# The first products of eight stages from the high parts of x alone, ahead of the fourth transposes, and tile 20's down products together ahead of tile 21's

## The chip, the cores and the metric

The kernel runs on one core of one Trainium2 chip. The metric is the device time of one execution in microseconds, lower is better. TensorE is called PE here, ScalarE ACT, VectorE DVE, GpSimd POOL; SP issues the transfers.

## What is computed

A block of the first kind and two of the second, on one sequence of 256 tokens with 1024 features, in float32:

```
x = x + 0.5 * swiglu(rms_norm(x))            # FFN a        norm 0
x = x + hybrid_mixer(rms_norm(x))            # mixer        norm 1
x = x + 0.5 * swiglu(rms_norm(x))            # FFN b        norm 2
x = rms_norm(x)                              #              norm 3
for i in (0, 1):
    # for i = 1: keys and values of MLA from x first (shared_kv)
    x = layer_norm(ALPHA * x + 0.5 * swiglu(x))          # FFN c, e     norms 4, 8
    x = layer_norm(ALPHA * x + mix(x))                   # FoX / MLA    norms 5, 9
    x = layer_norm(ALPHA * x + 0.5 * swiglu(x))          # FFN d, f     norms 6, 10
    x = layer_norm(ALPHA * x + sigmoid(x @ w_gate + b) * (p[i] @ w_proj))   # norms 7, 11

swiglu(x) = (silu(x @ w_gate_half) * (x @ w_up_half)) @ w_down    # hidden width 2752 or 2816
```

## The kernel before

**Split products.** A float32 product is made of three products of rounded operands: a tensor is split into a high part (`_hi`, an ACT copy) and what is left of it (`_lo`, a DVE subtraction), and hi x hi, hi x lo and lo x hi are added in PSUM. This holds for the weights (`w_hi`, `w_lo`, made from the landed `w_raw` by `split_hi` L308 and `split_lo` L315, in pieces of 1024 columns, in places 512) and for the activations.

**Stages.** Every engine has a program of its own, written out in order; semaphores tie them. Norm n ends in a turn: `x` is normalised in four pieces p = 0 to 3 (block b = p % 2 of 128 tokens, half p // 2 of the features), by `dve_rms_apply` (L537) or `dve_ln_apply` (L545, L548). PE transposes each piece with four transposes (`pe_turn`, L367) into banks 4, 6, 5 and 7; ACT copies each bank to `xT_hi` (`act_turn`, L471), DVE makes `xT_lo` (L557). Eight of the norms are followed by a stage whose first step is changed: FFN a to f, the mixer and FoX. In four of them ACT scales the whole of `x` by ALPHA after the fourth copy (`act_scale`, L476) - FFN c, d, e, f - and so it does in FoX.

**An FFN.** 22 tiles of 128 hidden features. `gate_up(i)` makes 48 products of 256 columns (`feature_major`, L343) over the eight k tiles of features; for tile 0 they come in a front (k 0 to 3) and a back half (k 4 to 7). ACT and DVE make the hidden tile from it (`silu` L487, product L575, high L491, low `hT_lo` L577). `down(i)` adds 12 products of 512 columns (`token_major`, L352) onto four accumulators, `psum[2 * b + half]` for block b and half of the features. `down(i - 1)` stands behind `gate_up(i)`, so that the hidden tile is made meanwhile. Behind the FFN, DVE adds each accumulator to `x` (`dve_add`, L524), ACT squares the halves (L457), and DVE and POOL make the factor of the norm (L512, L514, L601).

**Weights.** The chunk of tile i + 1 is split while tile i is worked on. In ACT's order at a stage's start stand: the four copies, the scaling, the last piece of chunk 0 (the down weights), pieces 0 and 1 of chunk 1, then `silu` of tile 0. The other pieces of chunk 0 are split during the stage before, except in FFN a, where they follow the fourth copy.

Of the kernel before, what the change touches and what calls it, by code (L numbers as in the profile page):

```python
# [16 lines left out]
P = 128  # L17
# [192 lines left out]
def build(nc, t, out):  # L210
    with ExitStack() as ctx:
# [149 lines left out]
        def pe_turn(n, src):  # L361
            for p in range(4):
# [7 lines left out]
        def pe_ffn(f, n):  # L370
# [21 lines left out]
            def down(tiles):  # L392
                for b in range(TB):
                    for half in range(2):
                        for i in tiles:
                            c = at + i
                            wait_split(pe, c, GU, FF_COLS)
                            pe.wait_ge(h_lo_made, FF_TILES * f + i + 1)
                            s = i % 2
                            ins = token_major(psum[2 * b + half][:, :], w_hi[chunks[c].pair], w_lo[chunks[c].pair],  # L400
                                              lambda j: GU + 512 * half, 512, (0,), lambda k: hT_hi[s], lambda k: hT_lo[s],
                                              b, i == 0, i == FF_TILES - 1)
                        if len(tiles) == 2:
                            ins.then_inc(acc_made, 1)
                if len(tiles) == 1:
                    ins.then_inc(down_made, 1)
# [40 lines left out]
        def act_squares(n, src, mean, blocks=range(TB)):  # L447

            for b in blocks:
                if n == 0:  # L450
                    act.wait_ge(x_landed[b], 16)
# [99 lines left out]
        def dve_turn(n, apply, eps):  # L551
# [7 lines left out]
            for p in range(4):  # L559
                b, k0 = p % 2, p // 2 * 4  # L560
                if p < 2:
                    dve_mean(n, b, eps)
# [1593 lines left out]
```

## Time and profile before

| | |
|---|---|
| median of 3 runs | 1975.18 us (1971.28 to 1981.16) |
| the profiled execution | 1975.18 us, its span 1973.9 us |
| PE busy | 1798.7 us, 91% of the span |
| DVE busy | 1088.8 us, 55% |
| ACT busy | 887.7 us, 45% |
| HBM | 298.52 MB read, 152 GB/s over the span |

The span is the stretch from the profile's first to its last instruction; the execution's time has 1.3 us around it. A busy share is an average over all stages: an engine that is at 91% may be the bound in most of them and idle at each border between two.

### The profile page before, as it was taken

The numbers are of one execution on the slowest core, as the hardware profiler recorded it, in microseconds if no ns is written. First come the engines' busy times: TensorE is split into PE (matmuls) and PEld (weight loads), VectorE is DVE, ScalarE is ACT, GpSimd is POOL, SyncE is SP. The second block draws the span as 40 slices with busy tenths as digits, with TensorE's granted clock in tenths as the row PEclk, the third lists the DMA queues.
The fourth block names the chain that finished last, engine by engine and source line by source line (L and its number), as shares of the span: only waits on it lengthen the run. The fifth ranks groups of instructions, "written<-read, shape, count | busy, mean of one in ns | idle before, by whom it ended". The sixth has DMA issues, their size and how long they took to land.

```text
span 1973.9 us, 27882 instructions
## 1 busy us (share of the span) xinstructions
PE 1798.7 (91%) x11764; PEld 1608.9 (82%) x11764; DVE 1088.8 (55%) x1696; ACT 887.7 (45%) x1515; POOL 105.1 (5%) x116
## 2 busy tenths in 40 slices
PE   7999897888999899988989999789997888899985
PEld 6999877666999799978868998579997667699974
DVE  5545555994554554554755555564556455455455
ACT  4444543344444444435645444454444444444443
POOL 0000001231000000001210000100000000100000
PEclk9999997999999999999999999889998999899997
DMA  8555340006555455525335554345543222454531
GB/s 318 182 189 182 107 173 33 1 1 242 188 181 189 150 194 190 192 98 192 131 125 197 192 186 177 117 156 192 192 157 141 77 96 75 167 201 181 192 107 43
DMA packets 31964, 301.38 MB, mean 153 GB/s; under 512 B 3792, under 2 KB 4320, under 8 KB 5984
## 3 DMA queue, kind: packets, MB, share of 16 engines
q1 hardware_dynamic: 31840, 299.60, 41.9%
q8 instruction: 93, 1.52, 0.3%
q14 instruction: 31, 0.25, 0.0%
HBM read 298.52 MB, written 1.06 MB: 152 GB/s over the span
## 4 chain that ended last, share of the span: by engine, by line
PE 78%; DVE 13%; ACT 5%; issue 2%; POOL 1%; DMA 0%; SPq 0%; DVEq 0%; ACTq 0%
PE bank L343 44%; PE bank L352 29%; DVE w_lo L315 2%; ACT w_hi L308 1%; DVE x L548 1%; PE bank L367 1%; POOL rstd L601 1%; DVE w_raw L1071 1%; DVE w_raw L1141 1%; DVE xT_lo L557 1%; DVE w_raw L1090 1%; ACT w_raw L913 1%; DVE w_raw L1076 1%; PE bank L787 1%; DVE mla_nm L1266 1%
## 5 line engine op out<-in xcount | busy, mean ns | idle before, releaser
L315 DVE TENSOR_TENSOR w_lo<-w_raw,w_hi 128x1024 fp32r<-128x1024 f32 (+4 forms) x545 | 608.5, 1170 | 386.2 <-ACT w_hi L308 385.5
L343 PE MATMUL bank<-xT_hi,w_hi 128*128 128x256 f32 x2392 | 685.9, 287 | 10.4 <-DVE w_lo L315 8.4
L343 PE MATMUL bank<-xT_lo,w_hi 128*128 128x256 f32 x2392 | 681.9, 285 | 0.0
L343 PE MATMUL bank<-xT_hi,w_lo 128*128 128x256 f32 x2392 | 681.5, 285 | 0.0
L308 ACT ACTIVATE w_hi<-w_raw 128x1024 fp32r<-128x1024 f32 (+4 forms) x561 | 523.7, 996 | 258.1 <-PE bank L352 258.0
L343 PEld LDWEIGHTS bank<-xT_hi,w_hi 128*128 128x128 f32 x2392 | 464.2, 194 | 22.6 <-DVE w_lo L315 10.1
L343 PEld LDWEIGHTS bank<-xT_lo,w_hi 128*128 128x128 f32 x2392 | 464.1, 194 | 5.7
L343 PEld LDWEIGHTS bank<-xT_hi,w_lo 128*128 128x128 f32 x2392 | 463.9, 194 | 0.0
L352 PE MATMUL bank<-w_hi,hT_hi 128*128 128x512 f32 x528 | 208.9, 396 | 7.4 <-DVE hT_lo L577 7.4
L487 ACT ACTIVATE ff_silu<-bank 128x256 f32<-128x256 f32 x132 | 51.0, 387 | 358.2 <-PE bank L343 358.0
L352 PE MATMUL bank<-w_hi,hT_lo 128*128 128x512 f32 x528 | 208.6, 395 | 0.0
L352 PE MATMUL bank<-w_lo,hT_hi 128*128 128x512 f32 x528 | 208.5, 395 | 0.0
L575 DVE TENSOR_TENSOR ff_silu<-ff_silu,bank 128x256 f32<-128x256 f32 x132 | 55.8, 422 | 204.8 <-ACT ff_silu L487 204.6
L352 PEld LDWEIGHTS bank<-w_hi,hT_hi 128*128 128x128 f32 x528 | 99.6, 189 | 28.0 <-issue 9.9
L352 PEld LDWEIGHTS bank<-w_lo,hT_hi 128*128 128x128 f32 x528 | 99.0, 187 | 23.9
L352 PEld LDWEIGHTS bank<-w_hi,hT_lo 128*128 128x128 f32 x528 | 98.9, 187 | 18.0
L352 PE MATMUL bank<-w_hi,xT_hi 128*128 128x256 f32 (+3 forms) x272 | 92.3, 339 | 9.9 <-DVE xT_lo L557 4.8
L577 DVE TENSOR_TENSOR hT_lo<-ff_silu,hT_hi 128x256 fp32r<-128x256 f32 x132 | 56.1, 425 | 64.0 <-ACT hT_hi L491 64.0
L352 PE MATMUL bank<-w_hi,xT_lo 128*128 128x256 f32 (+3 forms) x272 | 91.1, 335 | 0.0
L352 PE MATMUL bank<-w_lo,xT_hi 128*128 128x256 f32 (+3 forms) x272 | 91.0, 334 | 0.0
L601 POOL TENSOR_TENSOR rstd<-rstd,minus_half 128x1 f32<-128x1 f32 x24 | 21.5, 896 | 1288.0 <-DVE rstd L514 1288.0
L491 ACT ACTIVATE hT_hi<-ff_silu 128x256 fp32r<-128x256 f32 x132 | 55.2, 418 | 64.5 <-DVE ff_silu L575 64.5
(290 smaller groups left out, 1887.1 us busy)
## 6 DMA issues: line engine op xcount, KB each, us to landing
w_raw<-in_ffn_a SPq DMA_DIRECT2D x22, 1536.0 KB, 6.8
w_raw<-in_ffn_b SPq DMA_DIRECT2D x22, 1536.0 KB, 6.7
w_raw<-in_ffn_c SPq DMA_DIRECT2D x22, 1536.0 KB, 6.7
w_raw<-in_ffn_d SPq DMA_DIRECT2D x22, 1536.0 KB, 6.6
w_raw<-in_ffn_e SPq DMA_DIRECT2D x22, 1536.0 KB, 6.6
w_raw<-in_ffn_f SPq DMA_DIRECT2D x22, 1536.0 KB, 6.7
gains<-in_gains SPq DMA_DIRECT2D x11, 1024.0 KB, 5.6
w_raw<-in_mla_up SPq DMA_DIRECT2D x8, 1280.0 KB, 5.4
```

Source lines behind the costliest of these rows:

```text
L308: nc.scalar.activation(w_hi[c.pair][:, a:b], raw[c.slot][:, a:b], ACTF.Copy).then_inc(w_hi_made, 1)
L315: nc.vector.tensor_tensor(w_lo[c.pair][:, a:b], raw[c.slot][:, a:b], w_hi[c.pair][:, a:b].bitcast(F32), ALU.subtract).then_inc(w_lo_made, 1)
L343: ins = nc.tensor.matmul(o, w[:, c], a[:, k, :], start=(n == 0), stop=(n == last))
L352: ins = nc.tensor.matmul(o, a(k)[:, tok_of(b)], w[:, c], start=(first_k and n == 0), stop=(last_k and n == 3 * len(ks) - 1))
L367: ins = nc.tensor.transpose(bank[:, i * P:(i + 1) * P], src[:, b, (k0 + i) * P:(k0 + i + 1) * P], ident)
L487: nc.scalar.activation(sig[s][:, :], psum[4 + i % 4][:, 0:SEQ], ACTF.Silu).then_inc(silu_made, 1)
L491: nc.scalar.activation(hT_hi[s][:, :], sig[s][:, :], ACTF.Copy).then_inc(h_hi_made, 1)
L548: nc.vector.scalar_tensor_tensor(xb, xb, rstd[:, b:b + 1], gains[:, D + c.start:D + c.stop], ALU.mult, ALU.add).then_inc(normed, 1)
L557: nc.vector.tensor_tensor(lo, got, hi.bitcast(F32), ALU.subtract).then_inc(xT_lo_made, 1)
L575: nc.vector.tensor_tensor(sig[s][:, :], sig[s][:, :], up[:, SEQ:2 * SEQ], ALU.mult).then_inc(h_made, 1)
L577: nc.vector.tensor_tensor(hT_lo[s][:, :], sig[s][:, :], hT_hi[s][:, :].bitcast(F32), ALU.subtract).then_inc(h_lo_made, 1)
L601: nc.gpsimd.tensor_tensor(rstd[:, b:b + 1], rstd[:, b:b + 1], expo[:, 0:1], ALU.pow).then_inc(rooted, 1)
```

## The change

**At a stage's start** (`pe_first`, called by `pe_ffn` for tile 0 of each FFN, by `pe_mixer` and by `pe_fox`; `pe_turn` is no longer called ahead of these). PE transposes pieces 0, 1, 2. Then it makes, for the front half of the features, all products with `xT_hi`: w_hi and w_lo. Then it transposes piece 3, and makes the front products with `xT_lo`, the back ones with `xT_hi`, the back ones with `xT_lo`. The weights are waited for up to the half in question. The gate of tile 0 goes to bank 2 instead of bank 4, FoX's first tile to bank 0 instead of 6, as transposed pieces still stand in the banks used before. The number of products stays the same.

**In FFN a**, ACT and DVE split the first two pieces of chunk 0 ahead of the third copy and of the fourth normalised piece.

**At an FFN's end**, all of `down(20)`, block 1 first, stands behind `gate_up(21)`, and `down(21)` behind it. Before, tiles 20 and 21 alternated in each accumulator.

**Squares**: ACT waits for each half of a block by itself in norms 1 to 3.

```diff
-        def pe_turn(n, src):
-            for p in range(4):
+        def pe_turn(n, src, pieces=range(4)):
+            for p in pieces:
...
+        def pe_first(n, src, i, tiles):
+            hi, lo = w_hi[chunks[i].pair], w_lo[chunks[i].pair]
+            front, back = range(KD // 2), range(KD // 2, KD)
+
+            def of_high(ks):
+                wait_split(pe, i, 0, len(tiles) * P * (ks[-1] + 1))
+                for j, o in enumerate(tiles):
+                    for k in ks:
+                        c = slice((len(tiles) * k + j) * P, (len(tiles) * k + j + 1) * P)
+                        nc.tensor.matmul(o, hi[:, c], xT_hi[:, k, :], start=(k == 0), stop=False)
+                        nc.tensor.matmul(o, lo[:, c], xT_hi[:, k, :], start=False, stop=False)
+
+            def of_low(ks, signal=None):
+                for j, o in enumerate(tiles):
+                    for k in ks:
+                        c = slice((len(tiles) * k + j) * P, (len(tiles) * k + j + 1) * P)
+                        ins = nc.tensor.matmul(o, hi[:, c], xT_lo[:, k, :], start=False, stop=(k == KD - 1))
+                    if signal is not None:
+                        ins.then_inc(signal, 1)
+                return ins
+
+            def products(signal=None):
+                pe_turn(n, src, (0, 1, 2))
+                pe.wait_ge(xT_hi_made, 4 * n + 2)
+                of_high(front)
+                pe_turn(n, src, (3,))
+                pe.wait_ge(xT_lo_made, 4 * n + 2)
+                of_low(front)
+                pe.wait_ge(xT_hi_made, 4 * n + 4)
+                of_high(back)
+                pe.wait_ge(xT_lo_made, 4 * n + 4)
+                return of_low(back, signal)
+            return products
...
+                if i == 0:
+                    pe_first(n, src, c, (psum[2][:, 0:SEQ], psum[3][:, SEQ:2 * SEQ]))().then_inc(gate_up_made, 1)
+                    return
                 wait_split(pe, c, 0, GU)
-                if i == 0:
-                    for ks in (range(KD // 2), range(KD // 2, KD)):
-                        wait_xT(n, ks)
-                        feature_major(bank[:, 0:SEQ], hi, lo, lambda k: 2 * P * k, KD, xT_hi, xT_lo, ks)
-                        ins = feature_major(psum[3][:, SEQ:2 * SEQ], hi, lo, lambda k: 2 * P * k + P, KD, xT_hi, xT_lo, ks)
-                    ins.then_inc(gate_up_made, 1)
-                    return
...
             for i in range(FF_TILES):
                 gate_up(i)
                 if 1 <= i < FF_TILES - 1:
-                    down((i - 1,))
-            down((FF_TILES - 2, FF_TILES - 1))
+                    down(i - 1, 0)
+                    down(i - 1, 1)[1].then_inc(down_made, 1)
+
+            down(FF_TILES - 2, 1)
+            down(FF_TILES - 2, 0)
+            for b in range(TB):
+                for ins in down(FF_TILES - 1, b):
+                    ins.then_inc(acc_made, 1)
...
         def act_program():
             act_squares(0, x, False)
-            act_turn(0)
-            act_split(first["ffn_a"], 0, 4)
+            act_turn(0, (0, 1))
+            act_split(first["ffn_a"], 0, 2)
+            act_turn(0, (2, 3))
+            act_split(first["ffn_a"], 2, 4)
...
-            dve_turn(0, to_xn, RMS_EPS)
-            dve_split(first["ffn_a"], 0, 4)
+            dve_turn(0, to_xn, RMS_EPS, lambda: dve_split(first["ffn_a"], 0, 2))
+            dve_split(first["ffn_a"], 2, 4)
```

PE's order at the end of FFN b, behind `gate_up(21)`, before the change (`hT_hi0` is tile 20's hidden tile, `hT_hi1` tile 21's; banks 0 to 3 are the accumulators):

```order
L352 MATMUL bank0<-w_hi1,hT_hi0 128x512 [waits h_lo_made]
L352 MATMUL bank0<-w_hi1,hT_lo0 128x512
L352 MATMUL bank0<-w_lo1,hT_hi0 128x512
L352 MATMUL bank0<-w_hi0,hT_hi1 128x512 [waits h_lo_made,w_lo_made]
L352 MATMUL bank0<-w_hi0,hT_lo1 128x512
L352 MATMUL bank0<-w_lo0,hT_hi1 128x512
L352 MATMUL bank1<-w_hi1,hT_hi0 128x512
```

And with the change:

```order
L352 MATMUL bank2<-w_hi1,hT_hi0 128x512 [waits h_lo_made]
...
L352 MATMUL bank3<-w_hi1,hT_hi0 128x512
...
L352 MATMUL bank0<-w_hi1,hT_hi0 128x512
...
L352 MATMUL bank1<-w_hi1,hT_hi0 128x512
L352 MATMUL bank1<-w_hi1,hT_lo0 128x512
L352 MATMUL bank1<-w_lo1,hT_hi0 128x512
L352 MATMUL bank0<-w_hi0,hT_hi1 128x512 [waits h_lo_made,w_lo_made]
```

All 12 products of tile 20 now stand between `gate_up(21)` and the first that waits for tile 21's hidden tile; there were three.

PE's order at the start of FFN c, before (L367 are the transposes, bank 7 holds the fourth piece, banks 4 and 3 tile 0's gate and up):

```order
L367 MATMUL bank5<-const,x 128x128 [waits normed]
L367 MATMUL bank5<-const,x 128x128 x3
L367 MATMUL bank7<-const,x 128x128 [waits normed]
L367 MATMUL bank7<-const,x 128x128 x3
L343 MATMUL bank4<-xT_hi,w_hi1 128x256 [waits xT_lo_made,w_lo_made]
L343 MATMUL bank4<-xT_lo,w_hi1 128x256
L343 MATMUL bank4<-xT_hi,w_lo1 128x256
```

And with the change, from the third transposes (bank 5) on; L381 and L382 are the products of `xT_hi`, L388 those of `xT_lo`:

```order
L367 MATMUL bank5<-const,x 128x128 [waits normed]
L367 MATMUL bank5<-const,x 128x128 x3
L381 MATMUL bank2<-xT_hi,w_hi1 128x256 [waits w_lo_made,xT_hi_made]
L382 MATMUL bank2<-xT_hi,w_lo1 128x256
...
L381 MATMUL bank3<-xT_hi,w_hi1 128x256
L382 MATMUL bank3<-xT_hi,w_lo1 128x256
L367 MATMUL bank7<-const,x 128x128 [waits normed]
L367 MATMUL bank7<-const,x 128x128 x3
L388 MATMUL bank2<-xT_lo,w_hi1 128x256 [waits xT_lo_made]
L388 MATMUL bank2<-xT_lo,w_hi1 128x256 x3
L388 MATMUL bank3<-xT_lo,w_hi1 128x256 x4
L381 MATMUL bank2<-xT_hi,w_hi1 128x256 [waits w_lo_made,xT_hi_made]
```

The fourth transposes stood right behind the third; 16 products, all with the high part, now stand between them.

## Rows read from the trace of the kernel before

**Rows 1.** The page, part 4: the chain that ended last, by engine.

```profile
PE 78%; DVE 13%; ACT 5%; issue 2%; POOL 1%; DMA 0%; SPq 0%; DVEq 0%; ACTq 0%
```

**Rows 2.** The list of waits: engine, line, releaser; us in all, times, longest.

```profile
PE bank L343 <- DVE w_lo L315: 8.4, 5, 4.0
...
PE bank L352 <- DVE hT_lo L577: 7.4, 6, 1.2
```

**Rows 3.** Timeline of PE, end of FFN a: start us, us, what.

```profile
203.05 0.39 PE L352 MATMUL bank<-w_hi,hT_hi 128*128 128x512 f32 x1
...
203.52 0.39 PE L352 MATMUL bank<-w_lo,hT_hi 128*128 128x512 f32 x1
205.15 0.47 PE L352 MATMUL bank<-w_hi,hT_hi 128*128 128x512 f32 x1 [1.24 <-DVE hT_lo L577]
```

**Rows 4.** Timeline, the same FFN: last add and next stage's transposes.

```profile
210.31 0.69 DVE L524 SCALAR_TENSOR_TENSOR x<-bank,x 128x512 f32<-128x512 f32 x1 [0.70 <-PE bank L352]
...
212.81 0.44 PE L367 MATMUL bank<-const,xn 128*128 128x128 f32 x2 [2.55 <-DVE xn L537]
```

**Rows 5.** Timeline of PE, start of FFN c.

```profile
682.28 2.38 PE L367 MATMUL bank<-const,x 128*128 128x128 f32 x8 [1.01 <-DVE x L537]
685.47 1.11 PE L367 MATMUL bank<-const,x 128*128 128x128 f32 x4 [0.81 <-DVE x L537]
686.24 0.56 PE L343 MATMUL bank<-xT_hi,w_hi 128*128 128x256 f32 x1
686.60 0.41 PE L343 MATMUL bank<-xT_lo,w_hi 128*128 128x256 f32 x1
686.81 0.41 PE L343 MATMUL bank<-xT_hi,w_lo 128*128 128x256 f32 x1
...
692.95 0.28 PE L343 MATMUL bank<-xT_lo,w_hi 128*128 128x256 f32 x1
693.07 0.28 PE L343 MATMUL bank<-xT_hi,w_lo 128*128 128x256 f32 x1
693.64 0.35 PE L343 MATMUL bank<-xT_hi,w_hi 128*128 128x256 f32 x1 [0.29 <-DVE w_lo L315]
```

**Rows 6.** Windows table, FFN c: busy us by engine, granted clock, DMA share, GB/s.

```profile
682.30:688.60 6.30, 5.34 (x23) 4.54 (x24) 3.84 (x6) 3.17 (x4) 0.00 (x0) 0.50 0.28 117
```

**Rows 7.** Timeline of ACT, start of FFN c.

```profile
683.44 0.60 ACT L471 ACTIVATE xT_hi<-bank 128x512 fp32r<-128x512 f32 x1 [1.53 <-PE bank L367]
...
686.62 0.60 ACT L471 ACTIVATE xT_hi<-bank 128x512 fp32r<-128x512 f32 x1 [1.32 <-PE bank L367]
687.12 1.90 ACT L476 ACTIVATE x<-x 128x2048 f32<-128x2048 f32 x1
688.92 2.95 ACT L308 ACTIVATE w_hi<-w_raw 128x1024 fp32r<-128x1024 f32 x3
```

**Rows 8.** Timeline of DVE, end of FFN c, ahead of a layer norm.

```profile
873.45 0.69 DVE L524 SCALAR_TENSOR_TENSOR x<-bank,x 128x512 f32<-128x512 f32 x1 [1.12 <-PE bank L352]
...
875.78 0.16 DVE L531 SCALAR_TENSOR_TENSOR minus_mean<-row_sums,minus_mean 128x1 f32<-128x1 f32 x1
...
877.66 0.69 DVE L524 SCALAR_TENSOR_TENSOR x<-bank,x 128x512 f32<-128x512 f32 x1 [0.70 <-PE bank L352]
```

**Rows 9.** Timeline of PE, kernel's start: tile 0 of FFN a.

```profile
18.45 0.55 PE L343 MATMUL bank<-xT_hi,w_hi 128*128 128x256 f32 x1 [4.02 <-DVE w_lo L315]
```

**Rows 10.** Timeline of PE, start of FFN d: third and fourth transposes.

```profile
1038.71 1.12 PE L367 MATMUL bank<-const,x 128*128 128x128 f32 x4 [0.94 <-DVE x L548]
1040.76 1.11 PE L367 MATMUL bank<-const,x 128*128 128x128 f32 x4 [0.93 <-DVE x L548]
```

**Rows 11.** Timeline of PE, start of FFN e: fourth transposes, tile 1.

```profile
1294.56 1.11 PE L367 MATMUL bank<-const,x 128*128 128x128 f32 x4 [0.93 <-DVE x L548]
...
1303.11 0.28 PE L343 MATMUL bank<-xT_hi,w_hi 128*128 128x256 f32 x1
```

**Rows 12.** Timeline of PE, FoX: its first product.

```profile
889.66 0.58 PE L343 MATMUL bank<-xT_hi,w_hi 128*128 128x256 f32 x1 [1.41 <-DVE xT_lo L557]
```

More of the change, by code:

```diff
@@ L390, in gate_up, with down @@
                               range(KD)).then_inc(gate_up_made, 1)
[L392 to L406, printed above, removed]
+            def down(i, b):
+                c, s = at + i, i % 2
+                wait_split(pe, c, GU, FF_COLS)
+                pe.wait_ge(h_lo_made, FF_TILES * f + i + 1)
+                return [token_major(psum[2 * b + half][:, :], w_hi[chunks[c].pair], w_lo[chunks[c].pair],
+                                    lambda j: GU + 512 * half, 512, (0,), lambda k: hT_hi[s], lambda k: hT_lo[s],
+                                    b, i == 0, i == FF_TILES - 1) for half in range(2)]
             for i in range(FF_TILES):
@@ L449, in act_squares @@
             for b in blocks:
-                if n == 0:
-                    act.wait_ge(x_landed[b], 16)
-                elif mean:
-                    act.wait_ge(mean_made, 2 * (n - 4) + b + 1)
-                else:
-                    act.wait_ge(added, 4 * (n - 1) + 2 * b + 2)
-                for half in range(2):
+                for half in range(2):
+                    if n == 0:
+                        act.wait_ge(x_landed[b], 16)
+                    elif mean:
+                        act.wait_ge(mean_made, 2 * (n - 4) + b + 1)
+                    else:
+                        act.wait_ge(added, 4 * (n - 1) + 2 * b + half + 1)
                     ins = nc.scalar.activation(xn[:, b, half_of(half)], src[:, b, half_of(half)], ACTF.Square,
@@ L465, in turned_views, with act_turn @@
             return [z[:, k0:k0 + 4, tok_of(b)] for z in (xT_hi, xT_lo)] + [bank[:, :].rearrange("p (k t) -> p k t", t=P)]
-        def act_turn(n):
-            for p in range(4):
+        def act_turn(n, pieces=range(4)):
+            for p in pieces:
                 hi, _, got = turned_views(n, p)
@@ L486, in activate @@
                     act.wait_ge(h_lo_made, n0 + i - 1)
-                nc.scalar.activation(sig[s][:, :], psum[4 + i % 4][:, 0:SEQ], ACTF.Silu).then_inc(silu_made, 1)
+                gate = psum[2 if i == 0 else 4 + i % 4]
+                nc.scalar.activation(sig[s][:, :], gate[:, 0:SEQ], ACTF.Silu).then_inc(silu_made, 1)
                 act.wait_ge(h_made, n0 + i + 1)
@@ L562, in dve_turn @@
                     dve_mean(n, b, eps)
+                if p == 3:
+                    before_last()
                 apply(n, b, slice(k0 * P, (k0 + 4) * P))
@@ L690, in pe_mixer @@
         def pe_mixer():
-            i = first["nsa_a"]
-            hi, lo = w_hi[chunks[i].pair], w_lo[chunks[i].pair]
-            for ks in (range(KD // 2), range(KD // 2, KD)):
-                wait_xT(1, ks)
-                wait_split(pe, i, 0, 3 * P * (ks[-1] + 1))
-                for j in range(3):
-                    ins = feature_major(psum[j][:, 0:SEQ], hi, lo, lambda k: (3 * k + j) * P, KD, xT_hi, xT_lo, ks)
-                    if ks[0]:
-                        ins.then_inc(mix_tile, 1)
+            pe_first(1, xn, first["nsa_a"], [psum[j][:, 0:SEQ] for j in range(3)])(mix_tile)
             none = (mix_copied, 0)
@@ L1308, in pe_fox @@
         def pe_fox():
-            wait_xT(4, range(KD))
             none = (fox_tile, 0)
-            pe_features(first["fox_f"], [(psum[6][:, 0:SEQ], none)], fox_tile)
+            pe_first(4, x, first["fox_f"], [psum[0][:, 0:SEQ]])(fox_tile)
             tiles = lambda f0, f1: [(psum[7][:, 0:SEQ], f0), (psum[6][:, 0:SEQ], f1)]
@@ L1365, in act_fox @@
             act.wait_ge(small_landed, 16)
-            nc.scalar.activation(z_f[:, :], psum[6][0:FOX_H, 0:SEQ], ACTF.Identity, bias=small[0:FOX_H, HG + 1:HG + 2]).then_inc(fox_f_made, 1)
+            nc.scalar.activation(z_f[:, :], psum[0][0:FOX_H, 0:SEQ], ACTF.Identity, bias=small[0:FOX_H, HG + 1:HG + 2]).then_inc(fox_f_made, 1)
             act_split(first["fox_v"] + 1)
```

24 lines of the change are left out of this document (8 added, 16 removed).

## Prediction

> **What bounds the kernel now.** I read the page first: the chain that ended last is TensorE for 78% of the span and VectorE for 13% [rows 1]. TensorE (PE) is the bound inside the stages, and time can only be won where it stands idle between them. The list of waits gives the two idle places that the edit touches: six waits of 1.2 us for the last hidden tile, `hT_lo`, one at the end of each FFN, and five waits of `gate_up` for a weight split, `w_lo`, of which the longest, 4.0 us, is at the kernel's start [rows 2].
>
> Then the timeline. At an FFN's end the third product of tile 20 starts at 203.52, the next at 205.15. Products of 512 columns follow each other 0.235 us apart, so 1.40 us are empty (the profile counts 1.24 from the modelled end) [rows 3]. The last add starts at 210.31 and the first transposes of the next stage at 212.81 [rows 4].
>
> At the start of FFN c the second and third transposes stand in one row of eight from 682.28, the fourth in one from 685.47, and products follow at 686.24. Products are 0.21 us apart at first and 0.12 at the end [rows 5]; the granted clock from 682.3 to 688.6 is 0.50, the lower of the two levels, 1.2 GHz [rows 6]. After tile 0 PE waits: the last product starts at 693.07, tile 1 at 693.64, released by `w_lo` [rows 5]. What it waits for is a chain that starts at the fourth transposes: ScalarE (ACT) copies the fourth piece at 686.62, scales all of `x` for 1.90 us, then splits three weight pieces from 688.92 on [rows 7]. From the fourth transposes to tile 1 it is 8.17 us, whatever PE does meanwhile. This chain decides the edit.
>
> **The tail of an FFN (six places).** Now all 12 products of tile 20 stand ahead of the first of tile 21. They take 12 x 0.235 = 2.8 us. The hidden tile is there 2.1 us after tile 20's first product (203.05 to 205.15) [rows 3], so the wait disappears and PE ends 1.40 us sooner. The first accumulator comes 0.7 us later than before, the four then come every 0.70 us instead of every 1.40; VectorE's add takes 0.69 and keeps up [rows 8]. What releases the norm is the last add, as VectorE's order puts the variance behind it, so in the two RMS norms (before the mixer and FFN c) all of it moves by 1.40. The squares of half a block start with that half and stay hidden. In the four layer norms two small steps for the mean stand between the second and the third add: the second add, 1.40 behind the first of 873.45, ends at 875.54, the mean is done at 875.94 [rows 8]. The adds then start at T, T + 0.70, T + 1.70 and T + 2.31 (back to back an instruction starts some 0.08 before the modelled end of the one ahead, as the scaling does [rows 7]), where T is 873.45 + 0.71 = 874.16; the last starts at 876.47 instead of 877.66 [rows 8]: 1.19 sooner. Together 2 x 1.40 + 4 x 1.19 = **7.6 us won**. Bounds: 0, if the first accumulator led, and 8.4.
>
> **The kernel's start.** PE waits 4.02 us for the weight split there [rows 9]. Now two of the four pieces are split ahead of the third copy, the front products run in that wait, and the splits of the rest are in turn pushed behind them. Bounds are 0 and 4.0; I take **2.3 won**, a bit over half, as half of the products need only what is split early.
>
> **The fourth transposes.** PE works in order, so they now stand behind 16 products. In FFN c: the third transposes are issued by 684.3 (the row ends at 684.66, and a group of four occupies PE for 0.77, as from 685.47 to 686.24); the second high copy ends at 684.04 [rows 7], so products start at 684.3. At the low clock 16 of them take 16 x 0.213 = 3.4 us: fourth transposes at 687.7, 2.25 us later than before. ACT's copy, the scaling and the splits all move by it, and tile 1, which already waited on them, starts 2.25 us later. PE has less left to do (32 products, some 4 us), finishes tile 0 by 692.5 and then stands idle for 3.4 us. What was gained on PE is given back in this new wait. FFN d: 1038.71 + 0.77 + 3.41 = 1042.89 against 1040.76 [rows 10], +2.13. FFN f repeats d's rows: +2.1. FFN e: fourth transposes at 1294.56, tile 1 at 1303.11, which is 0.38 more than the chain's 8.17 [rows 11], so 2.13 less 0.38, +1.75. Together **+8.2**. At full clock the 16 products would take 1.9 us and the delay be about 0.5 per stage: bounds 2 and 9.
>
> Here the page "TensorE: Matmul & The Clock Gate" of the Trainium skill (Part 2: What happens when you issue a matmul) bears: weight loads may be pulled ahead, matmuls stay in program order. By it the transposes cannot pass the 16 products; were they able to, the 8.2 would be 0 and the sum about -9. No row of before shows a ready matmul behind a blocked one, so this is the page's word alone.
>
> FFN b has no scaling in its chain, so the chain is some 6.3 us, while PE's own work behind the transposes is 48 products, 5.8 at full and 10.2 at low clock; most of the delay is swallowed: **+0.3** (-0.5 to +1.5). In the mixer 24 products go ahead of the transposes and the back half needs a third split piece that is behind the fourth copy: **+0.4** (-0.5 to +1.2).
>
> FoX: PE waited 1.41 us for the fourth piece before its first product [rows 12]; this goes. But `fox_v` waits for copy, scaling and split of its own weights, the same chain. Eight products at low clock (1.7) plus 0.77 against the 2.05 between third and fourth transposes, as in rows 10: **+0.4**. The two other turned stages and the gates are not touched.
>
> **The clock.** After PE's 2.55 us of standing idle and sparse transposes the clock is at the low level [rows 4 to 6]. The new waits before tile 1 are 2 to 3.5 us, in FFN c, d, e, f and before `fox_v`. At low level a product costs 0.21 instead of 0.12, so each us of it loses 0.44 us. Lower bound 0 (stays full), upper bound that of FFN c's low stretch, 6.3 us [rows 6]: 2.8 each. I take 0.8 each, near the low end, as dense work stands on both sides of the wait: **+4.0**.
>
> **Sum.** -7.6 - 2.3 + 8.2 + 0.7 + 0.4 + 4.0 = +3.4 us. The profiled execution took 1975.18 us with a span of 1973.9; it is also the median of the three. So 1978.6.
>
> **Rivals.**
> (a) *The clock is early* (chance 0.2). Dense work now starts at the third transposes, 2.05 us earlier than before. If the clock is back while the 16 products run, the transposes are only 0.5 to 1 late (4 x 1.4 less), no wait reaches 2 us and the 4.0 goes too: 1978.6 - 5.6 - 4.0 = 1969. If it also saves 0.9 us of low clock in each of eight stages, 1962. The page named above (Part 1: The HAM clock gate) says that activity releases the throttle, which speaks for it; against it, the row of sparse transposes kept 0.50 until products ran, and the products ahead are themselves the activity, so they are slow first.
> (b) *The new wait drops the clock for long* (0.13), the slower one. Price 2.8 instead of 0.8 in five places: +10, 1988.6. It decides from 2.1 us per place (1.3 more than I take). For: the gap of 2.55 us did it. Against: that one was followed by sparse transposes.
> (c) *The tail gives nothing* (0.08), because the norm is led by the first accumulator or b0's squares: +7.6, 1986. Against: VectorE's order, last add before variance.
> (d) *The edit does not bite on the splits* (0.09): the chain has slack that I don't see, so that tile 1 starts when it did. Then -9.9 + 0.7: 1966. Against: three stages show the wait for `w_lo` itself.
>
> My own forecast, tail gains and split delays that roughly cancel, has 0.5. Half a per cent, 9.9 us, is about what a measurement of this kernel can tell from no change; the three runs of before themselves differ by that. Faster by more (below 1965.3): half of (a)'s further branch and a part of (d), 0.13. Slower by more (above 1985.1): (b) and half of (c), 0.16. The rest, 0.71, within. Range 1966 to 1987, from (d) to just beyond (c); (b)'s end and the far branch of (a) are left out.
>
> **What would show it.** Right: no row that waits for `hT_lo` at `token_major`; last add 1.4 (or 1.2) us after its place relative to the last `gate_up` of the FFN; in FFN c, d, f the fourth transposes 4.2 us after the third and tile 1 8.2 us after the fourth, with a PE wait of some 3 us for `w_lo`; the wait of 4.0 at the start shrunk to about 1 each at two places. Wrong, if products ahead of the fourth transposes are 0.12 apart, if ACT's splits don't wait for its fourth copy, or if the clock in the first us of tile 1 is 0.50 for longer than 3 us.

## The result, and the profile after

The changed kernel takes **1983.13 us** (median of 15 runs), the kernel before 1976.25 us (15 runs, 1971.11 to 1982.36). The ratio is 1.0038 with a 95% interval of 1.0027 to 1.0050: some 7 us slower, inside the half per cent that the prediction called no change, and inside its range. The interval stays clear of 1: this is a loss of 5 to 10 us, small but measured. The lowest of the 15 is 1977.44; one execution took 2926.71 us at a mean granted clock of 0.554 and is left out of the ratio.

The profiled execution of after took 1987.98 us with a span of 1986.7, against a span of 1973.9 before: 12.8 us apart. The profile of after is 4.9 us above its kernel's median, and that of before 1.1 us below its own. Where I count by stage I use these two profiles and say what of it is not the edit's.

The list of waits of after (engine, line, releaser: us in all, times, longest):

```profile
PE bank L343 <- DVE w_lo L315: 17.9, 7, 3.2
...
PE bank L352 <- DVE w_lo L315: 6.9, 3, 3.5
...
PE bank L381 <- DVE w_lo L315: 3.8, 3, 1.5
```

The wait for `hT_lo` [rows 2] is gone. The wait of L343 for the split has grown from 8.4 to 17.9 us. In both lists 3.2 us of it is one wait outside `gate_up`. The rest was mostly the 4.0 us at the kernel's start, and is now mostly four waits of 3.04 to 3.23 us ahead of tile 1 in FFN c, d, e and f. L352 waits for `w_lo` for 6.9 us instead of 3.3, as `fox_v` is now among it with 3.5, and the first products (L381) wait 3.8 us.

**The end of an FFN**, timeline of after, PE, end of FFN a (start, us, what):

```profile
202.54 0.39 PE L352 MATMUL bank<-w_hi,hT_hi 128*128 128x512 f32 x1
202.77 0.40 PE L352 MATMUL bank<-w_hi,hT_lo 128*128 128x512 f32 x1
...
205.11 0.40 PE L352 MATMUL bank<-w_lo,hT_hi 128*128 128x512 f32 x1
205.34 0.39 PE L352 MATMUL bank<-w_hi,hT_hi 128*128 128x512 f32 x1
...
207.91 0.40 PE L352 MATMUL bank<-w_lo,hT_hi 128*128 128x512 f32 x1
210.85 0.66 PE L367 MATMUL bank<-const,xn 128*128 128x128 f32 x4 [2.54 <-DVE xn L569]
```

24 products of 512 columns stand in one row with no hole. From the first of them to the next stage's transposes it is 8.31 us, where [rows 3, 4] give 203.05 to 212.81, 9.76: 1.45 us won.

**The start of FFN c**, the same view of after, to be held against [rows 5]:

```profile
677.43 2.37 PE L367 MATMUL bank<-const,x 128*128 128x128 f32 x8 [1.01 <-DVE x L569]
679.46 0.56 PE L381 MATMUL bank<-xT_hi,w_hi 128*128 128x256 f32 x1
679.82 0.42 PE L382 MATMUL bank<-xT_hi,w_lo 128*128 128x256 f32 x1
680.03 0.41 PE L381 MATMUL bank<-xT_hi,w_hi 128*128 128x256 f32 x1
...
682.80 0.41 PE L382 MATMUL bank<-xT_hi,w_lo 128*128 128x256 f32 x1
683.02 0.67 PE L367 MATMUL bank<-const,x 128*128 128x128 f32 x4
683.44 1.20 PE L388 MATMUL bank<-xT_lo,w_hi 128*128 128x256 f32 x8
...
686.38 1.12 PE L388 MATMUL bank<-xT_lo,w_hi 128*128 128x256 f32 x8
690.74 0.56 PE L343 MATMUL bank<-xT_hi,w_hi 128*128 128x256 f32 x1 [3.23 <-DVE w_lo L315]
691.09 0.41 PE L343 MATMUL bank<-xT_lo,w_hi 128*128 128x256 f32 x1
```

and ACT in the same stretch, to be held against [rows 7]:

```profile
683.72 0.60 ACT L502 ACTIVATE xT_hi<-bank 128x512 fp32r<-128x512 f32 x1 [3.28 <-PE bank L367]
684.21 1.90 ACT L507 ACTIVATE x<-x 128x2048 f32<-128x2048 f32 x1
686.02 2.94 ACT L308 ACTIVATE w_hi<-w_raw 128x1024 fp32r<-128x1024 f32 x3
```

The sixteen products ahead of the fourth transposes are 0.21 apart, the fourth transposes come 5.59 us after the row of eight (3.19 in [rows 5]), ACT waits 3.28 us for them, and tile 1 starts 14.98 us after the stage's first transposes (675.76) instead of 13.03. PE is through with tile 0 early and then stands idle for 3.23 us; and behind that its products are 0.21 us apart again, as at the lower clock.

The windows table of after for tile 1 of FFN b, c, d, e and f, each from its first product to the first `down` product (window and length; busy us and instructions of PE, PEld, DVE, ACT and POOL; granted clock, DMA share, GB/s):

```profile
490.70:496.52 5.82, 5.82 (x48) 5.82 (x49) 4.29 (x5) 3.26 (x4) 0.00 (x0) 1.00 0.78 291
690.74:699.23 8.49, 8.49 (x49) 8.49 (x49) 4.10 (x5) 3.26 (x4) 0.00 (x0) 0.64 0.83 328
1055.13:1062.45 7.32, 7.32 (x49) 7.32 (x49) 4.28 (x5) 3.26 (x4) 0.00 (x0) 0.77 0.84 319
1309.05:1317.31 8.26, 8.26 (x49) 8.26 (x49) 4.28 (x5) 3.26 (x4) 0.00 (x0) 0.66 0.86 323
1741.70:1748.84 7.14, 7.14 (x48) 7.14 (x49) 4.29 (x5) 3.26 (x4) 0.00 (x0) 0.79 0.82 305
```

Before, the same 48 products took 5.76 to 5.82 us in FFN c to f, at a clock of 1.00. After, only FFN b keeps it, behind a wait of 1.44 us; c, d, e and f follow waits of 3.04 to 3.23 us and lose 2.67, 1.51, 2.51 and 1.32 us.

Stage by stage, after less before, each counted inside its own stage:

| part | predicted | measured |
|---|---|---|
| six ends | -7.6 | -7.9 (1.45, 1.45, 1.20, 1.28, 1.27, 1.27) |
| kernel's start, first transposes to tile 1 | -2.3 | -1.5 (17.82 to 16.32) |
| later tile 1 in c, d, e, f | +8.2 | +7.4 (1.95, 2.23, 1.04, 2.14) |
| FFN b, mixer, FoX | +1.1 | +1.9 (0.6, 1.0, 0.3) |
| clock behind the new waits | +4.0 | +9.5 (8.0 in c to f, 1.5 in `fox_v`) |

The ends of FFN a, b, c and e are counted to the next stage's first transposes, those of d and f to the last add, as other work stands between there. The lines make +9.4. Of the 12.8 us between the two profiles, 0.9 is a later landing of the norm's gains at the very start (first transposes at 9.46, not 8.54). The other 2.5 us stand in stretches that the edit doesn't touch, and are a net of larger pieces: +4.1 in the MLA stage and +3.5 in the rest of FoX, -3.0 in the rest of the mixer, and smaller ones. So the table's lines are sound each for itself, but one pair of profiles can't confirm their sum.

### The profile page after: what moved, and what is told of

The parts are those of the page before. It is cut to its first block, busy times and chain, and to the rows that moved or that the text cites. A ratio compares the mean times of both kernels' runs of the same rounds, so it can differ in the third digit from the quotient of the medians.

```text
span 1986.7 us, 27884 instructions
## 1 busy us (share of the span) xinstructions
PE 1810.9 (91%) x11764; PEld 1625.1 (82%) x11764; DVE 1088.7 (55%) x1696; ACT 887.3 (45%) x1515; POOL 101.5 (5%) x116
## 4 chain that ended last, share of the span: by engine, by line
PE 77%; DVE 14%; ACT 5%; issue 2%; POOL 1%; DMA 0%; SPq 0%; DVEq 0%; ACTq 0%
PE bank L343 42%; PE bank L352 29%; DVE w_lo L315 3%; ACT w_hi L308 2%; DVE x L556 1%; DVE w_raw L1167 1%; PE bank L367 1%; DVE x L580 1%; DVE w_raw L1097 1%; POOL rstd L635 1%; DVE w_raw L1116 1%; PE bank L381 1%; PE bank L382 1%; ACT w_raw L939 1%; DVE xT_lo L589 1%
## 5 line engine op out<-in xcount | busy, mean ns | idle before, releaser
L343 PE MATMUL bank<-xT_hi,w_hi 128*128 128x256 f32 x2264 | 647.3, 286 | 18.5 <-DVE w_lo L315 17.9
L343 PE MATMUL bank<-xT_lo,w_hi 128*128 128x256 f32 x2264 | 643.9, 284 | 0.0
L343 PE MATMUL bank<-xT_hi,w_lo 128*128 128x256 f32 x2264 | 643.8, 284 | 0.0
L343 PEld LDWEIGHTS bank<-xT_hi,w_hi 128*128 128x128 f32 x2264 | 437.5, 193 | 30.3 <-DVE w_lo L315 19.7
L343 PEld LDWEIGHTS bank<-xT_lo,w_hi 128*128 128x128 f32 x2264 | 437.8, 193 | 5.7
L343 PEld LDWEIGHTS bank<-xT_hi,w_lo 128*128 128x128 f32 x2264 | 437.5, 193 | 0.0
L352 PE MATMUL bank<-w_lo,hT_hi 128*128 128x512 f32 x528 | 208.6, 395 | 0.0
L352 PE MATMUL bank<-w_hi,hT_lo 128*128 128x512 f32 x528 | 208.6, 395 | 0.0
L352 PE MATMUL bank<-w_hi,hT_hi 128*128 128x512 f32 x528 | 208.4, 395 | 0.0
L352 PEld LDWEIGHTS bank<-w_lo,hT_hi 128*128 128x128 f32 x528 | 99.0, 187 | 23.9
L352 PEld LDWEIGHTS bank<-w_hi,hT_hi 128*128 128x128 f32 x528 | 99.6, 189 | 18.4
L352 PEld LDWEIGHTS bank<-w_hi,hT_lo 128*128 128x128 f32 x528 | 98.9, 187 | 18.3
L352 PE MATMUL bank<-w_hi,xT_hi 128*128 128x256 f32 (+3 forms) x272 | 93.3, 343 | 13.6 <-DVE w_lo L315 6.9
L352 PE MATMUL bank<-w_hi,xT_lo 128*128 128x256 f32 (+3 forms) x272 | 92.0, 338 | 0.0
L352 PE MATMUL bank<-w_lo,xT_hi 128*128 128x256 f32 (+3 forms) x272 | 91.8, 337 | 0.0
```

The costliest lines, as they stand in the source:

```text
L343: ins = nc.tensor.matmul(o, w[:, c], a[:, k, :], start=(n == 0), stop=(n == last))
L352: ins = nc.tensor.matmul(o, a(k)[:, tok_of(b)], w[:, c], start=(first_k and n == 0), stop=(last_k and n == 3 * len(ks) - 1))
```

## The experiments

All kernels were timed against the kernel before on the same chip, in three groups, each on a chip of its own: experiments 1 to 4 in the first, where the kernel before took 1976.81 us, 5 to 7 and the first of 8 in the second (1977.69 us), the other two of 8 in the third (1976.09 us). "Below" and "above before" is between medians of one group. Versions of different groups, and the changed kernel itself, are best compared by their ratios to before. The intervals reach 3 to 5 us to either side, so neighbours in this list are often not told apart by their times, and then the rows of the profiles have to decide. My theory going in: the end of the FFN gains its 7.7 us whatever else is done; the start loses through one chain, fourth transposes, ACT's copy, scale, ACT's and VectorE's split, tile 1; and the clock falls in the wait that this chain makes. The rivals: the end only gains in combination, the split waits on something else, and tile 1 is longer for another reason than the clock.

**1. The new end alone.** The kernel before, with this in `pe_ffn`:

```diff
-            down((FF_TILES - 2, FF_TILES - 1))
+            down(FF_TILES - 2, 1)
+            down(FF_TILES - 2, 0)
+            for b in range(TB):
+                for ins in down(FF_TILES - 1, b):
+                    ins.then_inc(acc_made, 1)
```

> The kernel before with the new end of the FFN stages alone (tile 20 of token block 1 in the wait for tile 21). Theory (two independent parts, the end gains as in the trace of after: 1.45 us in each of two stages that an RMSNorm follows, 1.2 us in each of four others): the time falls by 7.7 us, ratio to before about 0.996, and the rows of every stage's first tile read as before. Rival 1 (the later 24 products only move the wait of the norm onto the weights' splits of the next stage): within 1 us of before. Rival 2 (the end gains only together with the new start, whose waits hide it): slower or the same.

Measured: 1965.63 us, 11.2 below before, ratio 0.9955 (0.9935 to 0.9975). The interval reaches from 5 to 13 us, so it holds the 7.7. In the profiles the span falls by 9.7: 7.7 at the six ends, and 2.0 net elsewhere, where no instruction is changed (the largest pieces are 1.9 less behind the mixer's start and 1.9 more behind FoX's). Both rivals are out: the end is a gain that stands by itself.

**2. The new start alone.** The changed kernel with the old `down` and its two-tile end.

> The changed kernel with the old end of the FFN stages: the products of the high parts ahead of the fourth transposes stand alone. Theory: the loss of the start is all there and nothing offsets it, 7 us of after plus 7.7 us of the ends: some 14 to 15 us slower than before, ratio about 1.0075; the waits ahead of tile 1 are 3.0 to 3.2 us in FFN c, d, e and f as in after. Rival (the new end itself costs, by its order of blocks, and the start is neutral): within 3 us of before.

Measured: 1988.84 us, **12.0 above** before, ratio 1.0065 (1.0043 to 1.0088). A little less than expected, and on the side of the theory: the start is a loss, and in the changed kernel the ends pay for most of it. The two parts add up to +0.8 us, where the changed kernel has +6.9; with some 4 us to either side of each part that is no contradiction, but no proof either that they simply add. Tile 1 in this kernel, windows of FFN c, d, e and f:

```profile
690.37:696.19 5.82, 5.82 (x48) 5.82 (x49) 4.10 (x5) 3.26 (x4) 0.00 (x0) 1.00 0.81 303
1050.66:1057.92 7.26, 7.25 (x49) 7.26 (x49) 4.29 (x5) 3.26 (x4) 0.00 (x0) 0.78 0.83 315
1307.57:1315.91 8.34, 8.34 (x48) 8.34 (x49) 4.28 (x5) 3.26 (x4) 0.00 (x0) 0.66 0.85 332
1736.44:1743.76 7.32, 7.32 (x49) 7.32 (x50) 4.29 (x5) 3.26 (x4) 0.00 (x0) 0.77 0.83 321
```

The waits ahead of them are 3.23, 3.14, 3.23 and 3.01 us. Three times the clock fell; in FFN c, behind the same 3.23 us as in after, it did not. So the price of such a wait is not fixed.

**3. The wait filled.** The changed kernel, with 24 products behind tile 0 of FFN c to f whose result nobody reads:

```diff
                     pe_first(n, src, c, (psum[2][:, 0:SEQ], psum[3][:, SEQ:2 * SEQ]))().then_inc(gate_up_made, 1)
+                    if n >= 3:
+                        for k in range(24):
+                            nc.tensor.matmul(psum[6][:, 0:SEQ], xT_hi[:, k % 8, 0:P], xT_hi[:, k % 8, :],
+                                             start=(k == 0), stop=(k == 23))
```

> The changed kernel with 24 extra products of 256 columns (their result is not used) behind tile 0 of FFN c, d, e and f, where TensorE otherwise waits 3.0 to 3.2 us for the weights' splits. Tile 1 still waits for the same split, so it starts no earlier; only the idle time goes. Theory (the wait makes the granted clock fall, and the low clock lengthens tile 1 by 1.5 to 2.7 us in each of these stages): tile 1 takes 5.8 us in the four stages, no stretch of low clock behind it, and the time is 6 to 9 us below after, near before. Rival (tile 1 is longer because of what ACT and VectorE do beside it, not the clock): tile 1 stays at 7.3 to 8.5 us and the time at that of after. Rival 2 (the extra products run over, into tile 1): slower than after by 2 us for each stage where they do.

Measured: 1974.38 us, 2.4 below before, ratio 0.9985 (0.9971 to 0.9999); after is 1.0038 (1.0027 to 1.0050), so 96 products of no use make the changed kernel some 9 to 10 us *faster*. PE at the start of FFN c in this kernel:

```profile
686.54 3.04 PE L419 MATMUL bank<-xT_hi 128*128 128x256 f32 x24
689.93 0.36 PE L343 MATMUL bank<-xT_hi,w_hi 128*128 128x256 f32 x1 [0.35 <-DVE w_lo L315]
690.12 0.28 PE L343 MATMUL bank<-xT_lo,w_hi 128*128 128x256 f32 x1
```

and its windows for tile 1 of FFN c and e:

```profile
689.93:695.75 5.82, 5.82 (x48) 5.82 (x49) 4.11 (x5) 3.27 (x4) 0.00 (x0) 1.00 0.81 309
...
1304.02:1309.85 5.83, 5.83 (x49) 5.83 (x49) 4.30 (x5) 3.26 (x4) 0.00 (x0) 1.00 0.78 298
```

Tile 1 still waits for the split in FFN c, e and f (0.35 or 0.36 us). ACT and VectorE do beside it what they did, and it takes 5.82 or 5.83 us again in all four stages. It starts 14.44 us after the first transposes in FFN c (after's 14.98), because the clock came back sooner in tile 0 there and the fourth transposes came 0.5 us earlier; in d, e and f it starts within 0.1 us of after's. What lengthened tile 1 in after was the clock, and the clock fell because PE stood idle.

**4. All transposes first.** The changed kernel, high products still ahead of low ones:

```diff
-                pe_turn(n, src, (0, 1, 2))
+                pe_turn(n, src, range(4))
                 pe.wait_ge(xT_hi_made, 4 * n + 2)
                 of_high(front)
-                pe_turn(n, src, (3,))
```

> The changed kernel with all four groups of transposes ahead of tile 0's first products again; the products of the high parts still come before those of the low parts, and the new end stays. Theory (the loss is the fourth transposes' delay, which passes through ACT's copy and scale to the split that tile 1 waits for, and what the clock costs behind that wait): the wait ahead of tile 1 falls from 3.2 us to under 1 us, tile 1 begins 13 to 14.5 us after the third-to-last stage's first product as before, the ends' gain stays: 7 to 9 us faster than before, ratio 0.996. Rival (the order of high and low products or the other bank of the gate makes the wait): it stays at 3 us, and the time at that of after.

Measured: 1962.19 us, **14.6 below** before, ratio 0.9934 (0.9912 to 0.9955). No wait of 0.3 us or more is left ahead of tile 1 in any FFN; the wait for `w_lo` in L343 falls from after's 17.9 us to 3.4, of which 3.2 is the one outside `gate_up`. One line moved back turns a loss of 7 us into a gain of 15. The gain is larger than I wrote (7 to 9): against the kernel with the new end alone, 3.4 us are the kernel's first stage, from the first transposes to the first `down` product 20.31 us against 23.71. PE's rows there:

```profile
14.39 1.12 PE L367 MATMUL bank<-const,xn 128*128 128x128 f32 x4 [1.71 <-DVE xn L568]
15.16 0.56 PE L381 MATMUL bank<-xT_hi,w_hi 128*128 128x256 f32 x1
...
22.96 0.28 PE L343 MATMUL bank<-xT_hi,w_hi 128*128 128x256 f32 x1
```

Against them, after's own start, where the back half waits 1.05 us for a split that stands behind ACT's copy of the late fourth piece (19.53, behind transposes of 18.44):

```profile
14.89 0.55 PE L381 MATMUL bank<-xT_hi,w_hi 128*128 128x256 f32 x1 [1.16 <-DVE w_lo L315]
...
18.44 1.06 PE L367 MATMUL bank<-const,xn 128*128 128x128 f32 x4
...
22.20 0.36 PE L381 MATMUL bank<-xT_hi,w_hi 128*128 128x256 f32 x1 [1.05 <-DVE w_lo L315]
```

**5. The order of conversions alone.** What of that 3.4 us is the products' order, and what the order in which ACT and VectorE convert? The kernel before with the new end, all transposes first, old order of products, and:

```diff
-            act_turn(0)
-            act_split(first["ffn_a"], 0, 4)
+            act_turn(0, (0, 1))
+            act_split(first["ffn_a"], 0, 2)
+            act_turn(0, (2, 3))
+            act_split(first["ffn_a"], 2, 4)
...
-                wait_split(pe, c, 0, GU)
+                if i > 0:
+                    wait_split(pe, c, 0, GU)
...
                         wait_xT(n, ks)
+                        wait_split(pe, c, 0, 2 * P * (ks[-1] + 1))
...
-            dve_turn(0, to_xn, RMS_EPS)
-            dve_split(first["ffn_a"], 0, 4)
+            dve_turn(0, to_xn, RMS_EPS, lambda: dve_split(first["ffn_a"], 0, 2))
+            dve_split(first["ffn_a"], 2, 4)
```

> The kernel before with the new end, and in the kernel's first stage the changed order of ACT's and VectorE's work (half of the weights' split between the halves of the turned input) with a wait for each half of the split; the products keep the old order, high and low together, behind all transposes. Theory (what the start gains is the order of the conversions, since the split of the weights is what TensorE waits for there, 4.02 us): stage a starts as fast as in the version with the transposes first (20.3 us from the first transposes to the first down product, against 23.7 us with the new end alone), time near 1962 us. Rival (the high products first are what fills the wait for the low part of the input): 1 to 3 us of the 3.4 us are missing, 1963.5 to 1965.5 us.

Measured: 1962.39 us, ratio 0.9928 (0.9904 to 0.9953); the first stage takes 19.87 us. That is all of the 3.4 us: with the transposes first, high products ahead of low ones bring nothing that shows, and the start's gain is that two pieces of the weights are converted early and are waited for by halves. Which of these two counts for how much was not tried.

**6. Half as many products ahead.** The changed kernel, with the first tile's 8 high products ahead of the fourth transposes and the rest behind them:

```diff
-            def of_high(ks):
+            def of_high(ks, which=range(len(tiles))):
...
                 for j, o in enumerate(tiles):
+                    if j not in which:
+                        continue
...
-                of_high(front)
+                of_high(front, (0,))
                 pe_turn(n, src, (3,))
+                of_high(front, range(1, len(tiles)))
```

> The changed kernel with only the first tile's 8 high products (in FFN: the gate's) ahead of the fourth transposes; the other 8 follow behind them. Theory (the delay of the fourth transposes is the products that stand ahead of them, at 0.21 us each, and the clock falls only behind the long wait): the fourth transposes come some 1.7 us earlier than in after, the waits ahead of tile 1 fall from 3.0 to 3.2 us to some 1.4 us, tile 1 takes 5.8 us again as in FFN b of after behind its wait of 1.44 us, and the time is about 12 us below after (4 us of delay and 8 us of clock), near 1972 us. Rival (the clock falls behind any wait of about 1 us): only the 4 us, near 1979 us. Rival 2 (half as many products do not move the split, for the split waits on something else): as after.

Measured: 1968.60 us, 9.1 below before, ratio 0.9952 (0.9936 to 0.9968), 3 us better than I wrote. Its windows for tile 1 of FFN b to f:

```profile
486.00:491.83 5.83, 5.83 (x49) 5.83 (x49) 4.33 (x5) 3.27 (x4) 0.00 (x0) 1.00 0.81 293
684.73:692.04 7.31, 7.31 (x48) 7.31 (x49) 4.11 (x5) 3.26 (x4) 0.00 (x0) 0.77 0.84 320
1044.87:1050.69 5.82, 5.82 (x48) 5.82 (x49) 4.29 (x5) 3.26 (x4) 0.00 (x0) 1.00 0.75 289
1296.40:1303.58 7.18, 7.17 (x48) 7.18 (x49) 4.30 (x5) 3.26 (x4) 0.00 (x0) 0.78 0.85 311
1724.48:1730.30 5.82, 5.82 (x48) 5.82 (x49) 4.29 (x5) 3.27 (x4) 0.00 (x0) 1.00 0.79 287
```

The waits ahead of them are 0.47, 1.96, 1.22, 2.26 and 1.37 us. The clock fell behind 1.96 and 2.26, waits shorter than I had expected to do it, and not behind the other three. Something I had not foreseen: FFN b (17.39 us from the first transposes to the first `down` product) and the mixer (45.20 to its first out product) are now *shorter* than with all transposes first (18.47 and 47.79; 18.46 and 47.26 in run 5).

**7. The scale of the residual behind the split.** The changed kernel, with ACT's 1.90 us scale taken out of the chain:

```diff
-            act_scale(3)
-            act_ffn(2, 2)
+            act_ffn(2, 2, 3)
...
                     split_hi(at + i + 1, 0)
                     split_hi(at + i + 1, 1)
+                    if i == 0 and n is not None:
+                        act_scale(n)
```

> The changed kernel with ACT's scale of the residual (1.90 us, between the copy behind the fourth transposes and the split that tile 1 waits for) moved behind two pieces of that split, in FFN c, d, e and f and in FoX. Theory (the split is the end of the chain fourth transposes, ACT copy, ACT scale, ACT split, VectorE split): the waits fall from 3.2 us to about 1.3 us, tile 1 begins as early as before the change or earlier, and the clock stays up: 8 us of chain and 8 us of clock below after, near 1967 us. Rival (the split waits for VectorE or for a transfer, not for ACT's order): waits stay at 3 us and the time at that of after. Rival 2 (the clock falls behind the shorter wait too): near 1975 us.

Measured: 1964.91 us, 12.8 below before, ratio 0.9932 (0.9909 to 0.9956), against 1.0038 for after. ACT in FFN c of this kernel:

```profile
682.24 0.60 ACT L502 ACTIVATE xT_hi<-bank 128x512 fp32r<-128x512 f32 x1 [3.29 <-PE bank L367]
682.73 2.95 ACT L308 ACTIVATE w_hi<-w_raw 128x1024 fp32r<-128x1024 f32 x3
685.58 1.89 ACT L507 ACTIVATE x<-x 128x2048 f32<-128x2048 f32 x1
```

The waits ahead of tile 1 are 1.44, 1.43, 1.24 and 1.26 us, 1.6 to 2.0 shorter than in after, tile 1 takes 5.82 to 5.83 in all four stages at a clock of 1.00, and ACT still waits 3.29 us for the late transposes. The chain is the one I had drawn. Take 1.9 us out of it, and tile 1 starts 1.79, 1.86, 0.99 and 1.73 us sooner after the stage's first transposes, and the clock's part goes as well. (In FFN e PE was itself through with tile 0 later here, so less of the shorter wait arrives.)

**8. Combinations.** All transposes first and the scale late:

> All four groups of transposes first, the new end, and the scale of the residual behind the split: the best candidate. Theory (in the version with the transposes first the split is in time already, except in FoX, where TensorE waits 1.04 us for it): only that wait goes, 0 to 1.5 us below the version without the late scale, near 1961.5 us. Rival (the scale is late for the products that use it at the end of the split, or the copies' order delays h of tile 0): 1 to 3 us slower than that version.

Measured: 1961.93 us, ratio 0.9919 (0.9895 to 0.9942); as expected, hardly more is left for the late scale to gain than FoX's wait (its start 12.07 us, 13.24 without). The starts of FFN d and f are 0.65 and 0.53 us shorter too: f's last wait of 0.20 us ahead of tile 1 is gone, and in d, where there was none, the clock came back sooner.

Eight products ahead (as in 6) and the scale late:

> Only the first tile's 8 high products ahead of the fourth transposes, with the scale of the residual behind the split, and the new end. In the run with 8 products the mixer's start took 45.2 us and FFN b's 17.4 us from the first transposes to the first down or output product, against 47.3 and 18.5 us with all transposes first; FFN c to f lost 0.5 to 2.4 us behind waits of 1.2 to 2.3 us for the split. Theory (8 high products ahead gain 1 us where the split is in time, and the late scale takes 1.8 us off the split): c, d, e, f each 0.5 to 1 us shorter than with all transposes first, the mixer 2 us, b 1 us: 4 to 7 us below that version with its late scale (1961.9 us), near 1956 us. Rival (the gain of the mixer and b was the clock's chance in one run): 1960 to 1963 us.

Measured: **1955.65 us**, 20.4 below before, ratio 0.9895 (0.9870 to 0.9919): the best version. PE in FFN c:

```profile
670.53 2.38 PE L367 MATMUL bank<-const,x 128*128 128x128 f32 x8 [0.81 <-DVE x L574]
672.57 0.56 PE L383 MATMUL bank<-xT_hi,w_hi 128*128 128x256 f32 x1
...
674.42 1.06 PE L367 MATMUL bank<-const,x 128*128 128x128 f32 x4
...
680.73 0.35 PE L343 MATMUL bank<-xT_hi,w_hi 128*128 128x256 f32 x1 [0.20 <-DVE w_lo L315]
```

The fourth transposes come 3.89 us after the row of eight (3.19 before, 5.59 in after), the eight products fill the gap ahead of them, and tile 1 waits 0.20 us. From the first transposes to the first `down` product FFN c takes 17.69 us, 18.55 with all transposes first; summed over all eight changed stages the two profiles differ by 6.1 us in these starts. The medians differ by 6.3 us, the ratios to before by 4.7 us, and the two intervals overlap (this one ends where the other has its middle). The mixer's start took 46.11 us here, not the 45.20 of run 6, at a granted clock of 0.93 against 0.96; the version of 1961.93 took 47.47 at 0.93. So 1.4 us of the mixer's gain is there at the same clock, and 0.9 is the clock's.

The same eight products in the mixer and FFN b alone, and all transposes first elsewhere:

> As the run before, but the 8 high products stand ahead of the fourth transposes in the mixer and in FFN b alone; the other stages have all transposes first. Theory: the 3 us of these two stages are gained, the rest is as with all transposes first and the late scale: near 1959 us, 2 to 4 us above the run with 8 products everywhere. Rival (the short waits that the 8 products leave in c to f cost more than they gain): at or below the run with 8 products everywhere.

Measured: 1963.09 us, ratio 0.9934 (0.9911 to 0.9956), a miss: I had expected 1959. The two starts did keep their gain (45.27 and 17.38 us), but the stretches behind FoX's start and behind MLA's (the attention ahead of FFN f), in which it has the same instructions as the version of 1961.93, took 143.72 and 208.50 us against 140.22 and 204.81: 7.2 us lost where nothing was changed, at granted clocks of 0.95 and 0.92 against 0.99 and 0.94. Why the clock differs there is open (below). That the eight products pay in FFN c to f as well rests on the starts of the version ahead: 3.4 of its 6.1 us are there. Their times alone don't show it, as such drift is as large.

## Why the prediction held, and where it was off

**The forecast of a change within half a per cent came true, and its two large terms stand as written:** the ends win about what the late splits lose. But the sum was not as good as that sounds. By stage it was to be +3.4 and is +9.4, six us further up, nearly all of it one term, the clock. The time, 1983.13 us, lies 4.5 us above the forecast and 2 us below the half per cent; the profiled execution, 1987.98 us, would have been outside the range. That the term's error fitted in is in part luck. The ends: -7.6 predicted, -7.9 measured, and the step from row to row (no wait for `hT_lo`, adds every 0.70 us, the last add releasing the norm) stands in the timeline as written; run alone they are a gain of 11 us (5 to 13).

**The fourth transposes' delay was right in mechanism and nearly in size,** 8.2 against 7.4. FFN e was mis-sized, 1.75 against 1.04: the clock came back while the products ran there (the last of the sixteen are 0.12 us apart), so its fourth transposes were 1.94 us late instead of 2.13, and from them to tile 1 it took 7.65 us, not 8.17. The rule of the Trainium skill that I cited there, that matmuls stay in program order (page "TensorE: Matmul & The Clock Gate", Part 2: What happens when you issue a matmul), can now be read off rows. VectorE has written the fourth piece at 679.82 + 0.74 = 680.56:

```profile
679.82 0.74 DVE L569 SCALAR_TENSOR_TENSOR x<-x,rstd,gains 128x512 f32<-128x512 f32 x1
```

and the transposes run at 683.02, 2.5 us later, behind the last of the sixteen products. The trace agrees with the rule.

**The mis-sized term is the clock,** +4.0 predicted, +9.5 measured. I priced each of five new waits at 0.8 us, "near the low end, as dense work stands on both sides of the wait". That argument failed: after 3 us of standing idle the dense work behind did start at 1.2 GHz (0.21 us from product to product), for 1.3 to 2.7 us of loss. The bound of 2.8 held. In FFN c and e the price was rival (b)'s; on the mean of five, 1.9, it stayed just under the 2.1 from which (b) decides. One of the signs that I had named for being wrong came true with it: the granted clock was to be 0.50 for at most 3 us of tile 1, and it was so for 6.1 us in FFN c, 5.6 in e, 3.5 in d and 3.0 in f. The filled waits show that this term is real: the kernel gains some 9 to 10 us by them, 8.0 of which the rows of tile 1 account for.

**The start was over-priced,** -2.3 against -1.5. I had said that the splits of the rest are pushed behind the front products, but not that the fourth piece's copy goes ahead of them and is itself late: the back half waits 1.05 us for it. With the transposes first the same stage shows what was there to win.

**The mixer** lost 1.0 where I took 0.4, by a wait of 1.55 us; FFN b's +0.6 and FoX's +0.3 are within what I gave.

Rival (a), the clock back early, is out as a whole: in FFN c the 16 products are 0.21 us apart to the last, and in e all but the last three. It happens in part, though, and not by the edit: in the run of the new start alone FFN c's fourth transposes came at 6.58 us after the first and not at 7.26, and its tile 1 kept the full clock. Rival (c), an end that gives nothing, fell with the run of the end alone; rival (d), an edit that doesn't bite on the splits, with the waits of 3.2 us. What I did not see at all was the middle way: fewer products ahead, which fill PE's gap between the third and the fourth transposes without outlasting it. [rows 5] had both numbers for it, a gap of 3.19 us less the 2 us of the row of eight, and 0.21 us a product.

## What to carry to other kernels

When an engine that works in order waits for its next input, put ahead of it only as much independent work as fits in the wait: past that, everything that other engines do with its output comes late, and the time saved reappears as a wait further on. Follow the output through every engine to whoever waits for it (here transposes, copy, scale, split, tile 1), and look there for work that only happens to stand in the chain; the scale was 1.9 us in five places. And test the two halves of a two-part change apart: here one was worth -11 us and the other +12 (each by some 4 us to either side), and together they looked like little.

## What was unexpected

- **Work of no use made the changed kernel some 9 to 10 us faster.** 24 unread products in each of four waits, 3.04 us each time, kept the granted clock at 1.00 and tile 1 at 5.82 us instead of 7.14 to 8.49.
- **The price of a wait varies.** Tile 1 of FFN b to f took 5.82 or 5.83 us behind waits of 0.35 to 1.44 us wherever I looked (13 windows of after and of the runs 3, 6 and 7), 7.31 and 7.18 behind 1.96 and 2.26, and 7.14 to 8.49 in seven cases of 3.01 to 3.23; but once, behind 3.23 us, 5.82.
- **Stretches with the same instructions differ between profiles.** The part from FoX's start to FFN d took 140.20 us before and 145.27 after, at granted clocks of 0.98 and 0.94, and the part from MLA's first product to FFN f 204.06 and 208.19, at 0.94 and 0.92:

```profile
893.25:1038.52 145.27, 134.02 (x850) 113.62 (x851) 86.34 (x191) 74.23 (x179) 25.69 (x37) 0.94 0.40 146
1516.98:1725.17 208.19, 178.89 (x971) 149.61 (x971) 101.83 (x240) 90.42 (x226) 8.18 (x9) 0.92 0.27 99
```

  (1.5 us of the first stretch's growth is the edit's, the slower `fox_v`.) Over the kernels here they range from 140.2 to 145.3 and from 203.0 to 208.5, the second with no relation to the edit. The lengths go with the granted clock. The stretch behind MLA's first product took 203.00 us at 0.95 in two kernels, 204.06 to 204.84 at 0.94, 206.34 and 206.48 at 0.93, and 208.19 and 208.50 at 0.92, so what drifts is the time that PE spends at the lower clock. That makes 4 or 5 us of one profile's difference accidental, and it is why I trust the stages' own rows more than a difference of spans. What makes the clock fall more often in one profile than in another, I did not settle.
